# Sixteen first-table panels move into the stretch in which the gates are made

## The chip, the cores and the metric

The kernel runs on one core of one Trainium2 chip. The metric is the device time of one execution in microseconds (us). Engines by their names in the profile: PE is TensorE (PEld its weight loads), DVE VectorE, ACT ScalarE, POOL GpSimd, SP SyncE; SP and POOL also issue the DMA transfers.

## The reference

Two layers over 256 tokens of width 2048: a Conformer convolution with a SwiGLU block, then a block of forgetting attention and pooling, and last a product-key expert layer ("peer"). Only that last layer matters here:

```python
# per token and head: 16 experts out of 128*128, with gates
v1, i1 = lax.top_k(s1, 16); v2, i2 = lax.top_k(s2, 16)
cand = v1[..., :, None] + v2[..., None, :]
top_s, top_pos = lax.top_k(cand, 16)
gates = softmax(top_s)
# per token: 8 heads * 16 experts
u = take(expert_u, idx); a = einsum('thkd,td->thk', u, x)
hid = gelu(a) * g
out = einsum('thk,thkd->td', hid, take(expert_v, idx))
```

## The kernel before

The expert layer takes the last 1130 us or so of the run. The experts' first key splits the work in two.

**Sparse part, first keys 0 to 87.** For each of 16 (token half, head) routes and each of 16 slots, `gather_u` fetches one row of 8 KB per token for 128 tokens by an indirect DMA, `dot` (L1706, on DVE, two halves of 1024) multiplies it with the token, `gelu` and `hidden` (L1756) give the weight, `spreads` (L1050, on ACT) lays it out, `gather_v` fetches the second table's row and `adds` (L2292, on PE) accumulates it. Rows whose first key is 88 or more are not fetched. The slots go in 64 groups of four. The U rows have 5 buffers, the V rows 7. POOL issues both kinds from one program order: U of slot k, then V of slot k-4. The U gather waits until the dot of slot k-5 is done, the V gather until PE has used the buffer (`v_used`).

**Dense part, first keys 88 to 127.** These 40 blocks are computed for all tokens. `dense_u_panel(d)` (L2240, PE, 16 products of 128x128 by 128x256) makes the dots of one block from a 1 MB panel that SP loads into one of two buffers (`raw`), `dense_hidden(d)` (L1060, ACT) writes the gelu into a row of `ha`. The gates of these blocks are made from one-hot rows: ACT makes `one_keys`, DVE `one_keys_2` and `one_keys_late`, `token_four(f)` (L2280, PE) multiplies them four tokens at a time, and `gated(group)` (L1749, DVE) multiplies `ha` with the gates of eight tokens, over all 40 blocks at once. `dense_v_panel(d)` (L2250, PE) then multiplies by a 1 MB panel of the second table.

**Order.** It is written out by hand. PE runs an iteration i of 0 to 64, in which the `adds` are those of group i-1; DVE and ACT run the loop over g. The U panels pass in i = 0 to 16 (three in each of i = 0 and 1, then 34 over 15 iterations), the transposed slots at i = 17, the 64 fours of tokens at i = 18 to 31 (eight in each of 18 and 19, then four), the residual at 33, the V panels from i = 34 to 60, three in two iterations. DVE also has the routing (top-k, L1639 to L1686) of 13 routes in groups 0 to 15; the groups 4, 9 and 14 have none. In PE's iteration a first panel stands ahead of the `adds`, a second behind two of them. SP's queue after the last U panel holds `xn_late`, `xres_late` and the V panels in this order; the first waits until all 40 U panels were used (L470), since it overwrites their moving operand.

Of the kernel before, what the change touches and what calls it, by code (L numbers as in the profile page):

```python
# [35 lines left out]

DENSE = 40
GATE_TOKENS = 8
SPARSE = NKEYS - DENSE
RMS_EPS, LN_EPS = 1e-6, 1e-5  # L40
LOWEST = -3.0e38
# [86 lines left out]

def dense_block(d):

    return d + 16 if d < 24 else d - 16 if d < 32 else d - 32


def score_row(th):
# [21 lines left out]
def u_panels_in(i):  # L156

    if i < 2:
        return range(3 * i, 3 * i + 3)
    return range(6 + 34 * (i - 2) // 15, 6 + 34 * (i - 1) // 15) if i < 17 else range(0)  # L160


def token_fours_in(g):
# [51 lines left out]
def two_layers(nc, stream, dense_u, columns, x, meta, b_out, g_mix_post, g_ffn, g_ffn_post, g_norm1, g_norm2, w_forget,  # L215
# [144 lines left out]
    pick = place("s_pick", [128, 2 * TOPK * TOPK], pick_at)  # L360
    cand = place("s_cand", [128, TOPK * TOPK], pick_at)
    cand_rest = place("s_cand_rest", [128, TOPK * TOPK], pick_at + 4 * TOPK * TOPK)
    iota_i = small("s_iota_i", NKEYS, mybir.dt.int32)
    iota_f = small("s_iota_f", NKEYS)
    sc_rest = small("s_sc_rest", NKEYS)
# [17 lines left out]
    with ExitStack() as ctx:  # L383
# [56 lines left out]
        v_loaded = [sem(f"v_loaded{i}") for i in range(NV)]  # L440
        dot_ready, dots_added, gelu_ready, hid_ready = sem("dot_ready"), sem("dots_added"), sem("gelu_ready"), sem("hid_ready")
        spread_ready, v_used = sem("spread_ready"), sem("v_used")
        acc_done, out_ready, stored = sem("acc_done"), sem("out_ready"), sem("stored")

        def four_tiles(b):
# [171 lines left out]
        def _(act):  # L617
# [435 lines left out]

            def dense_hidden(d):

                b = 4 + d % 4
                act.wait_ge(panel_used, NPANELS + 1 + d + 1)
                if d == 32:
                    act.wait_ge(expert_ready, PH)
                act.activation(ha[:, dense_block(d), :], bank[b][:, 0:T], ACT.Gelu_apprx_tanh).then_inc(bank_empty[b], 1)  # L1060

            def slots_transposed(t):

# [17 lines left out]
                act.wait_ge(distance_ready, turn + 1)  # L1081
                act.activation(four, four, ACT.Relu, scale=-1.0, bias=1.0).then_inc(one_key_ready, 1)

            slots_stored = [n.after(f"empty{6 + t}", DENSE // 4 + 1) for t in range(TT)]
            for g in range(ROUTES * GROUPS):
                if g == 18:
                    for t in range(TT):
# [17 lines left out]
        def _(dve):  # L1105
# [614 lines left out]
            def one_keys_2(m):  # L1720

                if m == 0:
                    for t in range(TT):
                        dve.wait_ge(bank_empty[6 + t], n.after(f"empty{6 + t}", DENSE // 4 + 1))
                wait(dve, one_key_used, 2 * (m - 2))
                first = 8 * m % 128
                columns = [slots_t[m // 16][:, kind * SLOTS + first:kind * SLOTS + first + 8].unsqueeze(2).to_broadcast([128, 8, DENSE])
                           for kind in (0, 2)]
                eight = one_key_2[:, m % 3 * 8 * DENSE:(m % 3 + 1) * 8 * DENSE].rearrange("p (t g) -> p t g", t=8)
                link(dve.tensor_tensor(eight, iota_f[:, SPARSE:].unsqueeze(1).to_broadcast([128, 8, DENSE]), columns[0], ALU.is_equal))  # L1730
                dve.tensor_tensor(eight, eight, columns[1], ALU.mult).then_inc(one_key_2_ready, 1)
# [6 lines left out]
                dve.tensor_tensor(one_key_late[:, :].rearrange("p (t k) -> p t k", t=8),  # L1738
                                  iota_f[:, :].unsqueeze(1).to_broadcast([128, 8, NKEYS]), keys_2, ALU.is_equal).then_inc(one_key_late_ready, 1)

            def gated(group):

                b = 6 + group % 2
                if group == 0:
                    for a in range(2):
                        dve.wait_ge(bank_empty[4 + a], n.after(f"empty{4 + a}", DENSE // 4))
                dve.wait_ge(one_key_used, GATE_TOKENS // 4 * (group + 1))
                some = ha[:, :, GATE_TOKENS * group:GATE_TOKENS * (group + 1)]
                dve.tensor_tensor(some, some, bank[b][:, 0:GATE_TOKENS * DENSE].rearrange("p (t g) -> p g t", t=GATE_TOKENS), ALU.mult)\  # L1749
                    .then_inc(bank_empty[b], 1)  # L1750

            def hidden(g):

# [44 lines left out]
            for g in range(ROUTES * GROUPS):  # L1798
                for turn in range(BATCH):
                    dot(g * BATCH + turn)  # L1800
                    if turn == 0 and g:
                        hidden(g - 1)
                        if route_in(g - 1):
                            gates_softmax(route_in(g - 1))
                    if route_in(g):
                        route(route_in(g), turn)
                    fours = token_fours_in(g)
                    for f in fours[turn * len(fours) // 4:(turn + 1) * len(fours) // 4]:
                        if f >= 4 and f % 2 == 0:
                            gated(f // 2 - 2)  # L1810
                        if f % 2 == 0:
                            one_keys_2(f // 2)
                        if f % 4 == 1:
                            one_keys_late(f // 4)
                    if g == 32 and turn < 2:
                        gated(T // GATE_TOKENS - 2 + turn)
                dots_summed(g)
                if g == 61:
                    for q in range(4):
                        result(0, q)  # L1820
# [6 lines left out]
        def _(pe):  # L1827
# [399 lines left out]

            def dense_u_panel(d):

                b = 4 + d % 4  # L2230
                if d == 0:
                    pe.wait_ge(xnt_ready, 1)
                into(b, d // 4)
                if d < NE:
                    pe.wait_ge(early_loaded[d], 16)
                else:
                    pe.wait_ge(raw_loaded[(d - NE) % 2], (NPANELS // 4 + (d - NE) // 2 + 1) * 16)
                source = panel_early[d] if d < NE else raw[(d - NE) % 2]
                for k in range(KT):
                    ins = pe.matmul(bank[b][:, 0:T], source[:, k * 128:(k + 1) * 128], xnt[:, k, 0:T], start=k == 0, stop=k == KT - 1)  # L2240
                ins.then_inc(panel_used, 1)
# [14 lines left out]
            def slots_transposed(t):  # L2256

                pe.wait_ge(gates_ready, PH * (t + 1))
                into(6 + t, DENSE // 4)
                for kind in range(3):  # L2260
                    ins = pe.transpose(bank[6 + t][:, kind * SLOTS:(kind + 1) * SLOTS], picked[t][:, kind * SLOTS:(kind + 1) * SLOTS], ident[:, :])
                ins.then_inc(bank_full[6 + t], 1)

            def token_four(f):

                b = 6 + f // 2 % 2
                if f % 2 == 0:
                    into(b, DENSE // 4 + 1 + f // 4)
                turn = 2 * (f // 4) + f % 4
                if f % 4 < 2:  # L2270
                    pe.wait_ge(one_key_ready, turn + 1)
                else:
                    pe.wait_ge(one_key_late_ready, f // 4 + 1)
                pe.wait_ge(one_key_2_ready, f // 2 + 1)
                four = one_key[:, turn % 4 * 4 * NKEYS:(turn % 4 + 1) * 4 * NKEYS] if f % 4 < 2 else \
                    one_key_late[:, f % 2 * 4 * NKEYS:(f % 2 + 1) * 4 * NKEYS]
                for e in range(4):
                    token = 4 * f + e
                    own_2 = slice(token % 24 * DENSE, (token % 24 + 1) * DENSE)
                    ins = pe.matmul(bank[b][:, token % GATE_TOKENS * DENSE:(token % GATE_TOKENS + 1) * DENSE], four[:, e * NKEYS:(e + 1) * NKEYS],  # L2280
                                    one_key_2[:, own_2], start=True, stop=True)
                ins.then_inc(one_key_used, 1)
# [19 lines left out]
            for i in range(ROUTES * GROUPS + 1):  # L2302
                for d in u_panels_in(i)[:1]:
                    dense_u_panel(d)
                if i == 17:
                    for t in range(TT):
                        slots_transposed(t)
                if i == 33:
                    for b in (4, 5):
                        into(b, DENSE // 4)  # L2310
                    for b in (6, 7):
                        into(b, DENSE // 4 + 1 + T // GATE_TOKENS // 2)
                    pe.wait_ge(xres_back, 16)
                    residual(1)
                for d in v_panels_in(i)[:1]:
                    dense_v_panel(d)
                for f in token_fours_in(i)[:-4]:
                    token_four(f)
                for q in range(4):
                    if i >= 1:  # L2320
                        adds(4 * (i - 1) + q)
                    if q == 1:
                        for d in u_panels_in(i)[1:2]:
                            dense_u_panel(d)
                        for d in v_panels_in(i)[1:]:
                            dense_v_panel(d)
                for d in u_panels_in(i)[2:]:
                    dense_u_panel(d)
                for f in token_fours_in(i)[-4:]:
                    token_four(f)  # L2330
# [70 lines left out]
```

## Time and profile before

| | |
|---|---|
| median of 3 runs | 3005.09 us (3003.09 to 3007.17) |
| the profiled execution's own time | 3004.93 us |
| its span, first to last instruction | 3002.9 us |
| busy: PE, PEld | 2736.4, 2038.3 us |
| busy: DVE, ACT, POOL | 1923.8, 1178.5, 668.0 us |
| moved by DMA | 785.5 MB |

Each row of the profile's engine table is busy time of that engine in one execution. Busy PE is time with a matmul under way, whatever its clock; the granted clock is a row of its own, in tenths of full speed (2.4 GHz) in the slices and as a fraction in stretches. The DMA share is the mean busy share of the 16 DMA engines.

### The profile page before, as it was taken

The numbers are of one execution on the slowest core, as the hardware profiler recorded it, in microseconds if no ns is written. First come the engines' busy times: TensorE is split into PE (matmuls) and PEld (weight loads), VectorE is DVE, ScalarE is ACT, GpSimd is POOL, SyncE is SP. The second block draws the span as 40 slices with busy tenths as digits, with TensorE's granted clock in tenths as the row PEclk, the third lists the DMA queues.
The fourth block names the chain that finished last, engine by engine and source line by source line (L and its number), as shares of the span: only waits on it lengthen the run. The fifth ranks groups of instructions, "written<-read, shape, count | busy, mean of one in ns | idle before, by whom it ended". The sixth has DMA issues, their size and how long they took to land.

```text
span 3002.9 us, 45413 instructions
## 1 busy us (share of the span) xinstructions
PE 2736.4 (91%) x17100; PEld 2038.3 (68%) x17100; DVE 1923.8 (64%) x3184; ACT 1178.5 (39%) x2298; POOL 668.0 (22%) x568
## 2 busy tenths in 40 slices
PE   8999999999999998999999999999976678888884
PEld 7886788888888887989999889777753322222220
DVE  6888566555656565455445558987769875555555
ACT  1003443334333344425334444645456642222232
POOL 0000000000000000040000002544448765454453
PEclk9999999999999998999999999999977779999886
DMA  6333545555555553443555657999999999999997
GB/s 244 140 141 111 206 157 185 187 191 183 194 182 193 184 192 122 155 152 141 182 182 182 248 199 250 372 418 408 415 375 408 397 409 417 409 420 391 411 409 300
DMA packets 131297, 785.51 MB, mean 262 GB/s; under 512 B 34630, under 2 KB 34630, under 8 KB 35846
## 3 DMA queue, kind: packets, MB, share of 16 engines
q1 hardware_dynamic: 55424, 393.68, 35.5%
q0 software_dynamic: 75712, 389.74, 32.3%
q8 instruction: 93, 1.52, 0.2%
q14 instruction: 68, 0.56, 0.1%
HBM read 940.23 MB, written 4.19 MB: 315 GB/s over the span
## 4 chain that ended last, share of the span: by engine, by line
PE 57%; DMA 20%; DVE 12%; issue 6%; ACT 3%; POOL 1%; DVEq 1%; POOLq 0%; SPq 0%; ACTq 0%
DMA s_u<-in_expert_u,s_u_index 17%; PE bank L1847 10%; PE bank L1841 10%; PE bank L1843 10%; PE bank L1842 10%; PE bank L1848 5%; PE bank L1937 4%; DVE s_u L1706 4%; PE bank L2240 4%; PE bank L2292 2%; DMA s_v<-in_expert_v,s_v_index 2%; DVE s_cacc L1217 2%; ACT s_spread L1050 2%; DVE s_w_lo L1128 1%; DVE s_yrow L1390 1%
## 5 line engine op out<-in xcount | busy, mean ns | idle before, releaser
L1128 DVE TENSOR_TENSOR s_w_lo<-s_raw,s_w_hi 128x2048 fp32r<-128x2048 f32 x258 | 592.6, 2297 | 577.8 <-ACT s_w_hi L628 577.4
L628 ACT ACTIVATE s_w_hi<-s_raw 128x2048 fp32r<-128x2048 f32 x256 | 490.5, 1916 | 750.9 <-PE bank L1843 475.4
L1847 PE MATMUL bank<-s_a,s_w_hi 128*128 128x512 f32 x1408 | 494.7, 394 | 3.2 <-DVE s_w_lo L1128 3.2
L2292 PE MATMUL bank<-s_v,s_spread 128*32 128x512 f32 x2048 | 302.8, 721 | 183.1 <-ACT s_spread L1050 115.9
L1706 DVE CUSTOM_DVE_ANT_0 s_u<-s_u,s_xn_late 128x1024 f32<-128x1024 f32 x256 | 303.8, 1224 | 246.8 <-DMA s_u<-in_expert_u,s_u_index 246.5
L1050 ACT ACTIVATE s_spread<-s_ident,s_hid 32x32 f32<-32x32 f32 x1024 | 325.6, 318 | 205.5 <-DVE s_hid L1756 188.0
L1848 PE MATMUL bank<-s_a,s_w_lo 128*128 128x256 f32 x1408 | 395.1, 281 | 0.0
L585 POOL DMA_INDIRECT s_u<-in_expert_u,s_u_index x256 | 300.0, 1172 | 416.4 <-DVE s_halfdot L1706 240.4
L601 POOL DMA_INDIRECT s_v<-in_expert_v,s_v_index x256 | 317.9, 1242 | 196.8 <-PE bank L2292 115.5
L1706 DVE CUSTOM_DVE_ANT_0 s_u<-s_u,s_xn 128x1024 f32<-128x1024 f32 x256 | 303.8, 1224 | 60.3 <-DMA s_u<-in_expert_u,s_u_index 59.3
L1841 PE MATMUL bank<-s_a,s_w_hi 128*128 128x256 f32 x1152 | 325.1, 282 | 3.4 <-DVE s_a L1152 1.8
L1842 PE MATMUL bank<-s_a,s_w_hi 128*128 128x256 f32 x1152 | 324.4, 282 | 0.0
L1843 PE MATMUL bank<-s_a,s_w_lo 128*128 128x256 f32 x1152 | 324.0, 281 | 0.0
L2292 PEld LDWEIGHTS bank<-s_v,s_spread 128*32 128x32 f32 x2048 | 62.9, 125 | 375.5 <-ACT s_spread L1050 135.4
L1847 PEld LDWEIGHTS bank<-s_a,s_w_hi 128*128 128x128 f32 x1408 | 264.7, 188 | 66.5 <-DVE s_w_lo L1128 6.4
L2250 PE MATMUL bank<-s_raw,s_ha 128*32 128x512 f32 x2560 | 295.5, 615 | 0.0
L2240 PE MATMUL bank<-s_xnt,s_raw 128*128 128x256 f32 x1184 | 264.7, 382 | 2.1 <-DMA s_raw<-in_dense_u 2.1
L1848 PEld LDWEIGHTS bank<-s_a,s_w_lo 128*128 128x128 f32 x1408 | 265.0, 188 | 0.4
L2240 PEld LDWEIGHTS bank<-s_xnt,s_raw 128*128 128x128 f32 x1184 | 222.1, 190 | 58.7 <-issue 29.1
L1937 PE MATMUL bank<-s_a_f,s_raw 128*128 128x272 f32 x1024 | 235.2, 393 | 2.9 <-DVE s_a_f L1185 2.1
L2250 PEld LDWEIGHTS bank<-s_raw,s_ha 128*32 128x32 f32 x2560 | 83.3, 115 | 215.1 <-issue 215.1
L1937 PEld LDWEIGHTS bank<-s_a_f,s_raw 128*128 128x128 f32 x1024 | 194.4, 190 | 43.4 <-issue 3.5
(321 smaller groups left out, 3809.8 us busy)
## 6 DMA issues: line engine op xcount, KB each, us to landing
s_raw<-in_stream SPq DMA_DIRECT2D x292, 1024.0 KB, 4.7
s_raw<-in_expert_v SPq DMA_DIRECT2D x40, 1024.0 KB, 8.9
s_raw<-in_dense_u SPq DMA_DIRECT2D x37, 1024.0 KB, 8.7
s_u<-in_expert_u,s_u_index POOLq DMA_INDIRECT x256, 17.4
s_v<-in_expert_v,s_v_index POOLq DMA_INDIRECT x256, 17.6
s_panel_early<-in_dense_u POOLq DMA_DIRECT2D x3, 1024.0 KB, 11.5
s_xres<-in_x SPq DMA_DIRECT2D x2, 1024.0 KB, 6.0
out<-s_out_row SPq DMA_DIRECT2D x32, 64.0 KB, 3.3
```

Source lines behind the costliest of these rows:

```text
L628: act.activation(w_hi[s % 2][:, :], raw[s][:, :], ACT.Copy).then_inc(hi_ready, 1)
L1050: ins = act.activation(spread[g % NW][s * Q:(s + 1) * Q, q, :], ident[own, own], ACT.Copy, scale=hid[g % NH][own, s:s + 1])
L1128: dve.tensor_tensor(w_lo[s % 2][:, :], raw[s][:, :], w_hi[s % 2][:, :].bitcast(f32), ALU.subtract)\
L1706: ins = dve.tensor_tensor_reduce(out=u_slot[k % NU][:, half], in0=u_slot[k % NU][:, half], in1=xn_late[:, half] if t else xn[:, 0, half], ...
L1841: pe.matmul(dst, left[0], right[0], start=start, stop=False)
L1842: pe.matmul(dst, left[0], right[1], start=False, stop=False)
L1843: return pe.matmul(dst, left[1], right[0], start=False, stop=stop)
L1847: pe.matmul(dst, left[0], both, start=start, stop=False)
L1848: return pe.matmul(dst[:, 0:T], left[1], both[:, 0], start=False, stop=stop)
L1937: ins = pe.matmul(bank[c][:, 0:L], raw[c % 4][:, k * 128:(k + 1) * 128], a_f[:, k, :], start=k == 0, stop=k == KT - 1)
L2240: ins = pe.matmul(bank[b][:, 0:T], source[:, k * 128:(k + 1) * 128], xnt[:, k, 0:T], start=k == 0, stop=k == KT - 1)
L2292: ins = pe.matmul(bank[4 * t + q][c * Q:(c + 1) * Q, :], spread[g % NW][:, q, :], v_slot[k % NV][:, c * 512:(c + 1) * 512], start=False, s ...
```

## The change

The first 24 panels pass in i = 0 to 16, the other 16 in i = 17 to 29, at 16 over 13 iterations. They use banks 4 and 5 alone, since banks 6 and 7 hold the gates by then. The gates of a group of tokens may now come before the gelu of some panels: `gated(group, missing)` copies the gates into those rows of `ha` (the late panels are rows 0 to 15, the last panel row 0) and multiplies the rest. When a late panel's gelu comes, ACT writes the tokens whose gates are already in place into one of two buffers `late_act`, the other tokens straight into `ha`, and DVE's `landed(d)` multiplies the two, at the first turn of group i+2.

```diff
+FIRST_U, LATE_U = 24, 16
...
     if i < 2:
         return range(3 * i, 3 * i + 3)
-    return range(6 + 34 * (i - 2) // 15, 6 + 34 * (i - 1) // 15) if i < 17 else range(0)
+    if i < 17:
+        return range(6 + (FIRST_U - 6) * (i - 2) // 15, 6 + (FIRST_U - 6) * (i - 1) // 15)
+    return range(FIRST_U + LATE_U * (i - 17) // 13, FIRST_U + LATE_U * (i - 16) // 13) if i < 30 else range(0)
...
+def u_bank(d):
+
+    if d < FIRST_U:
+        return 4 + d % 4, d // 4
+    return 4 + (d - FIRST_U) % 2, FIRST_U // 4 + (d - FIRST_U) // 2
+
+
+def gated_before(g):
+
+    fours = 8 * (g - 18) if g < 20 else 4 * (g - 16)
+    return max(0, min(fours, T // 4) // 2 - 2)
+
+
+LANDS_IN = {d: i + 2 for i in range(30) for d in u_panels_in(i) if d >= FIRST_U}
...
-                b = 4 + d % 4
+                b, late = u_bank(d)[0], d - FIRST_U
                 act.wait_ge(panel_used, NPANELS + 1 + d + 1)
-                if d == 32:
-                    act.wait_ge(expert_ready, PH)
-                act.activation(ha[:, dense_block(d), :], bank[b][:, 0:T], ACT.Gelu_apprx_tanh).then_inc(bank_empty[b], 1)
+                done = 0
+                if late >= 0:
+                    done = GATE_TOKENS * gated_before(LANDS_IN[d])
+                    if late == 0:
+                        act.wait_ge(expert_ready, TT * PH)
+                    wait(act, late_landed, late - 1)
+                    act.activation(late_act[:, late % 2, 0:done], bank[b][:, 0:done], ACT.Gelu_apprx_tanh)
+                act.activation(ha[:, dense_block(d), done:], bank[b][:, done:T], ACT.Gelu_apprx_tanh).then_inc(bank_empty[b], 1)
...
-                dve.tensor_tensor(some, some, bank[b][:, 0:GATE_TOKENS * DENSE].rearrange("p (t g) -> p g t", t=GATE_TOKENS), ALU.mult)\
-                    .then_inc(bank_empty[b], 1)
+                gates = bank[b][:, 0:GATE_TOKENS * DENSE].rearrange("p (t g) -> p g t", t=GATE_TOKENS)
+                if missing:
+                    dve.tensor_copy(some[:, 0:missing, :], gates[:, 0:missing, :])
+                dve.tensor_tensor(some[:, missing:, :], some[:, missing:, :], gates[:, missing:, :], ALU.mult).then_inc(bank_empty[b], 1)
+
+            def landed(d):
+
+                late, (b, k) = d - FIRST_U, u_bank(d)
+                groups = gated_before(LANDS_IN[d])
+                for group in (groups - 2, groups - 1):
+                    gates_taken = n.after(f"empty{6 + group % 2}", FIRST_U // 4 + 2 + group // 2)
+                    dve.wait_ge(bank_empty[6 + group % 2], gates_taken)
+                dve.wait_ge(bank_empty[b], n.after(f"empty{b}", k + 1))
+                some = ha[:, dense_block(d), 0:GATE_TOKENS * groups]
+                dve.tensor_tensor(some, some, late_act[:, late % 2, 0:GATE_TOKENS * groups], ALU.mult).then_inc(late_landed, 1)
...
-                    fours = token_fours_in(g)
+                    for d in range(FIRST_U, DENSE):
+                        if turn == 0 and LANDS_IN[d] == g:
+                            landed(d)
+                    fours, missing = token_fours_in(g), sum(LANDS_IN[d] > g for d in range(FIRST_U, DENSE))
                     for f in fours[turn * len(fours) // 4:(turn + 1) * len(fours) // 4]:
                         if f >= 4 and f % 2 == 0:
-                            gated(f // 2 - 2)
+                            gated(f // 2 - 2, missing)
```

The other edits set the banks' counts to the new number of panels. The two table layouts follow `dense_block`, so each panel is still 1 MB, and as many are loaded.

## Rows read from the trace of the kernel before

**Rows 1.** The page's 40 slices: PE, its granted clock, the DMA engines.
```profile
PE   8999999999999998999999999999976678888884
PEclk9999999999999998999999999999977779999886
DMA  6333545555555553443555657999999999999997
```
**Rows 2.** Windows over groups 2-15, 16-33 and 34-60: length, busy, clock, DMA.
```profile
core 0: us, PE busy (x) PEld busy (x) DVE busy (x) ACT busy (x) POOL busy (x), PEclk, DMA share, GB/s
1891.72:2169.78 278.06, 275.93 (x1460) 201.30 (x1453) 230.26 (x649) 152.53 (x490) 134.40 (x113) 1.00 1.00 411
2169.78:2450.03 280.25, 197.35 (x1248) 111.70 (x1250) 233.31 (x441) 162.99 (x493) 184.48 (x143) 0.74 0.98 396
2450.03:2932.43 482.40, 402.30 (x3416) 107.86 (x3412) 263.43 (x486) 142.94 (x459) 249.24 (x216) 0.91 1.00 410
```
**Rows 3.** Timeline of DVE: last instruction of groups 1 to 4, 20, 21 (start, us).
```profile
1891.72 0.16 DVE L1718 TENSOR_TENSOR s_adot<-s_halfdot 128x4 f32<-128x4 f32 x1
1911.78 0.15 DVE L1718 TENSOR_TENSOR s_adot<-s_halfdot 128x4 f32<-128x4 f32 x1
...
1931.85 0.15 DVE L1718 TENSOR_TENSOR s_adot<-s_halfdot 128x4 f32<-128x4 f32 x1
...
1941.83 0.17 DVE L1718 TENSOR_TENSOR s_adot<-s_halfdot 128x4 f32<-128x4 f32 x1
...
2263.94 0.16 DVE L1718 TENSOR_TENSOR s_adot<-s_halfdot 128x4 f32<-128x4 f32 x1
...
2277.20 0.17 DVE L1718 TENSOR_TENSOR s_adot<-s_halfdot 128x4 f32<-128x4 f32 x1
```
**Rows 4.** The chain that ended last, 1928 to 1937 us (start, us, what).
```profile
1928.00 7.10 PE bank L2240 x32
1935.11 1.85 PE bank L2292 x16
```
**Rows 5.** DMA by queue and issue: first 1850 to 1890 us, then 1890 to 2200.
```profile
s_u<-in_expert_u,s_u_index POOLq DMA_INDIRECT x8, 8.6
s_v<-in_expert_v,s_v_index POOLq DMA_INDIRECT x6, 6.4
...
q0 software_dynamic: 17815, 90.80, 71.7%
q1 hardware_dynamic: 4896, 35.65, 27.9%
...
s_u<-in_expert_u,s_u_index POOLq DMA_INDIRECT x64, 19.2
```
**Rows 6.** Timeline of PE, 2200 to 2254 us: the same work at both clocks.
```profile
2200.58 3.64 PE L2292 MATMUL bank<-s_v,s_spread 128*32 128x512 f32 x32
...
2223.90 5.50 PE L2292 MATMUL bank<-s_v,s_spread 128*32 128x512 f32 x32
...
2242.25 3.61 PE L2280 MATMUL bank<-s_one_key,s_one_key_late 128*128 128x40 f32 x16
...
2252.33 1.96 PE L2280 MATMUL bank<-s_one_key,s_one_key_late 128*128 128x40 f32 x16
```
**Rows 7.** Windows of 5 us (columns as in Rows 2), and a line of POOL's timeline.
```profile
2245.00:2250.00 5.00, 5.00 (x36) 1.79 (x36) 4.10 (x7) 0.00 (x0) 1.39 (x1) 0.68 0.48 195
2250.00:2255.00 5.00, 4.29 (x40) 3.65 (x32) 4.93 (x12) 1.86 (x7) 3.27 (x4) 1.00 0.74 241
...
2248.61 1.66 POOL L601 DMA_INDIRECT s_v<-in_expert_v,s_v_index  x1 [6.45 <-PE bank L2292]
```
**Rows 8.** Groups by line, 1850 to 3003 us (busy us, mean ns | idle before).
```profile
L1738 DVE TENSOR_TENSOR s_one_key_late<-s_iota_f,s_slots_t 128x1024 f32<-128x1024 f32 x16 | 19.5, 1219 | 2.6 <-PE bank L2280 2.6
L1749 DVE TENSOR_TENSOR s_ha<-s_ha,bank 128x320 f32<-128x320 f32 x32 | 15.4, 481 | 3.2 <-PE bank L2280 3.2
L1060 ACT ACTIVATE s_ha<-bank 128x256 f32<-128x256 f32 x40 | 13.4, 382 | 9.6 <-PE bank L2240 9.3
```

More of the change, by code:

```diff
@@ L129, in dense_block @@
 def dense_block(d):
-    return d + 16 if d < 24 else d - 16 if d < 32 else d - 32
+    return d + LATE_U if d < FIRST_U else DENSE - 1 - d
 def score_row(th):
@@ L362, in two_layers @@
     cand_rest = place("s_cand_rest", [128, TOPK * TOPK], pick_at + 4 * TOPK * TOPK)
+    late_act = place("s_late_act", [128, 2, T], pick_at)
     iota_i = small("s_iota_i", NKEYS, mybir.dt.int32)
@@ L442, in two_layers @@
         spread_ready, v_used = sem("spread_ready"), sem("v_used")
+        late_landed = sem("late_landed")
         acc_done, out_ready, stored = sem("acc_done"), sem("out_ready"), sem("stored")
@@ L1082, in one_keys @@
                 act.activation(four, four, ACT.Relu, scale=-1.0, bias=1.0).then_inc(one_key_ready, 1)
-            slots_stored = [n.after(f"empty{6 + t}", DENSE // 4 + 1) for t in range(TT)]
+            slots_stored = [n.after(f"empty{6 + t}", FIRST_U // 4 + 1) for t in range(TT)]
             for g in range(ROUTES * GROUPS):
@@ L1723, in one_keys_2 @@
                     for t in range(TT):
-                        dve.wait_ge(bank_empty[6 + t], n.after(f"empty{6 + t}", DENSE // 4 + 1))
+                        dve.wait_ge(bank_empty[6 + t], n.after(f"empty{6 + t}", FIRST_U // 4 + 1))
                 wait(dve, one_key_used, 2 * (m - 2))
@@ L1739, in one_keys_late, with gated @@
                                   iota_f[:, :].unsqueeze(1).to_broadcast([128, 8, NKEYS]), keys_2, ALU.is_equal).then_inc(one_key_late_ready, 1)
-            def gated(group):
+            def gated(group, missing):
                 b = 6 + group % 2
@@ L1745, in gated @@
                     for a in range(2):
-                        dve.wait_ge(bank_empty[4 + a], n.after(f"empty{4 + a}", DENSE // 4))
+                        dve.wait_ge(bank_empty[4 + a], n.after(f"empty{4 + a}", FIRST_U // 4))
                 dve.wait_ge(one_key_used, GATE_TOKENS // 4 * (group + 1))
                 some = ha[:, :, GATE_TOKENS * group:GATE_TOKENS * (group + 1)]
-                dve.tensor_tensor(some, some, bank[b][:, 0:GATE_TOKENS * DENSE].rearrange("p (t g) -> p g t", t=GATE_TOKENS), ALU.mult)\
-                    .then_inc(bank_empty[b], 1)
+                gates = bank[b][:, 0:GATE_TOKENS * DENSE].rearrange("p (t g) -> p g t", t=GATE_TOKENS)
[11 more added lines that the diff above has]
+                dve.tensor_tensor(some, some, late_act[:, late % 2, 0:GATE_TOKENS * groups], ALU.mult).then_inc(late_landed, 1)
             def hidden(g):
@@ L1815, in _ @@
                     if g == 32 and turn < 2:
-                        gated(T // GATE_TOKENS - 2 + turn)
+                        gated(T // GATE_TOKENS - 2 + turn, 0)
                 dots_summed(g)
@@ L2228, in dense_u_panel @@
             def dense_u_panel(d):
-                b = 4 + d % 4
+                b, k = u_bank(d)
                 if d == 0:
                     pe.wait_ge(xnt_ready, 1)
-                into(b, d // 4)
+                into(b, k)
                 if d < NE:
@@ L2258, in slots_transposed @@
                 pe.wait_ge(gates_ready, PH * (t + 1))
-                into(6 + t, DENSE // 4)
+                into(6 + t, FIRST_U // 4)
                 for kind in range(3):
@@ L2267, in token_four @@
                 if f % 2 == 0:
-                    into(b, DENSE // 4 + 1 + f // 4)
+                    into(b, FIRST_U // 4 + 1 + f // 4)
                 turn = 2 * (f // 4) + f % 4
@@ L2309, in _ @@
                     for b in (4, 5):
-                        into(b, DENSE // 4)
+                        into(b, FIRST_U // 4 + LATE_U // 2)
                     for b in (6, 7):
-                        into(b, DENSE // 4 + 1 + T // GATE_TOKENS // 2)
+                        into(b, FIRST_U // 4 + 1 + T // GATE_TOKENS // 2)
                     pe.wait_ge(xres_back, 16)
```

## The prediction

> **What bounds the kernel now.** I read the slices first, then the windows, then the timelines inside them. The slices show the expert layer (the last 15) with the DMA row at 9 and PE's clock down after 2200 us [rows 1]. The change touches two stretches of it. *Front*, groups 2 to 15, 278.06 us; *middle*, groups 16 to 33, 280.25 us. The third, groups 34 to 60, it leaves alone. The windows show a DMA share of 1.00, 0.98 and 1.00 in the three [rows 2]. PE is busy for 275.93 of 278.06 us in the front, and for 197.35 of 280.25 at a granted clock of 0.74 in the middle. DVE stands at 230 and 233 us.
>
> So three resources are close in the front. Each alone would take:
> - PE: back to back, a panel 7.10 us and the 16 products behind it 1.85 [rows 4]. Per group 31/14 panels and 32 `adds` products: 2.21 x 7.10 + 3.7 = 19.4 us. It is nearly the 19.9 us that a group lasts (278.06 / 14).
> - DVE: groups 1 to 3, all with routing, last 20.06 us each; group 4, without, 9.98 [rows 3]. Groups 2 to 15 have 11 with routing and 3 without (4, 9, 14): 220.7 + 29.9 = 250.6 us.
> - DMA: queue q1 moved 35.65 MB, 34 panels of 1.05 MB, in 4896 packets, 144 each, for 27.9% of 310 us: 2.54 us of all 16 engines per panel. Queue q0 had 17815 packets, at 144 each 123.7 gathers, for 71.7%: 1.80 us per gather, 14.4 us per group of eight [rows 5]. Front: 14 x 14.4 + 31 x 2.54 = 280.3 us against 278.06 measured. Middle: 18 x 14.4 + 7 x 2.54 (three U panels, xn_late, xres_late, two V panels) = 277.0 against 0.98 x 280.25 = 274.6. The working closes to 1%.
>
> DMA thus explains the length of both stretches; PE explains the front as well, but not the middle.
>
> **The change, part by part.**
> *Transfers.* Nothing is removed: as many gathers and as many 1 MB panels. Of 31 U panels in the iterations of the front 16 stay; 15 x 2.54 = 38.1 us of transfer go to the middle (there 3 become 18). If DMA never idled before or after, the end would not move at all. What counts is idle DMA.
>
> *Front.* DMA's work falls to 278 - 38 = 240 us, PE's to 14 x 3.7 + 16 x 7.10 = 165 us. DVE's stays at 250.6 and is now the largest: the front can't be shorter than that, and it gets DVE for its bound. I take 253, since groups differ. While DVE is the bound, DMA gets ahead, but only as far as the buffers go. How far, I read from issue to landing: 19.2 us under a full queue, 8.6 us just before, at 1850 to 1890, where DVE paced the groups [rows 5]. The queue holds 19.2 - 8.6 = 10.6 us less at the front's end: that much of the transfers is done earlier. 240 + 10.6 = 250.6, as much as DVE needs; so DMA idles for some 2 us only.
>
> *Middle.* 274.6 + 38.1 - 10.6 = 302.1 us of transfer, plus idle. Before, idle was 2% of 280, 5.6 us, most of it in one place: the V gather at 2248.61 was held 6.45 us by PE, and the share was 0.48 and 0.74 in the two 5 us windows there [rows 7]. PE was late because it had waited for the first one-hot rows and then worked at half clock. With a panel in each of those iterations PE fills that wait and its clock may hold: 16 L2280 products take 1.96 us at full and 3.61 at half clock, 32 L2292 3.64 and 5.50 [rows 6]. That would give 2 to 3 us back. Against it, the four 1 MB transfers that followed the last U panel are no longer there to fill the gap, and PE is tighter. I take 6 us of idle: 308 us.
>
> *PE in the middle.* Per group of 18 to 29: 32 L2280 products 3.9, `adds` 3.7, 16/13 panels 8.7, together 16.3 us, against DMA's 14.4 + 1.23 x 2.54 = 17.5. It fits at full clock, with 1.2 us to spare.
>
> *DVE in the middle.* At its own pace a group there takes it 13.26 us (group 21) [rows 3]. From the two widths 1024 in 1219 ns and 320 in 481 ns [rows 8], an operation costs about 0.15 us fixed and 1.05 ns per element. `landed` runs 16 times over 16 to 224 tokens, 2128 elements in all: 16 x 0.15 + 2.2 = 4.6 us, with its waits some 6. Splitting `gated` adds the fixed part 28 times: 4.2 us. The sum is 10 us over 13 groups, 0.8 each: 14.1, under 17.5; free while DMA paces. `landed` stands at the first turn of group i+2 and waits for ACT's gelu of a panel that PE passed in iteration i. Behind it stand the next dot, the gates and, through `dot_ready`, POOL's gathers. PE runs panel i before the `adds` of i-1, which themselves wait for group i on DVE, so it has about a group (17 us) in hand: nothing, unless PE falls behind. The overwritten buffer (`late_landed`) is freed in the same turn in which ACT needs it; under 1 us of ACT.
>
> *ACT.* 16 more gelus, at most 0.38 each [rows 8], 6 us over 13 groups; ACT is busy 163 of 280 us [rows 2]. Free.
>
> *Queues.* SP: sixteen loads come later, and behind them xn_late, xres_late and the first two V panels. The last U panel passes in iteration 29, xn_late is needed in group 32; two groups (35 us) against 19.2 us of landing at worst [rows 5]. Free. POOL's order is untouched.
>
> *Sum.* 253 + 308 = 561 against 558.3 now: +2.7 us. On the profiled execution (span 3002.9, its time 3004.93) that is 3007.6; the median of the runs is 0.16 above it, so **3007.8**. Bounds: with no lead over from the front, the middle has 312.7 + 6 and the sum is +13.4. With a larger lead (17 us) the front itself becomes DMA's, 257, and the sum +0.4; with no idle left, -5.6.
>
> **The rivals.**
> *A, PE is what bounds the front, and the middle has room.* For it: PE's 99% of the front at full clock, 70% of the middle. The front falls by 27.4 us to DVE's 250.6; the middle takes the panels in at less than their 2.54 us, because its clock and its order leave DMA 396 GB/s where the front had 411 [rows 2]. At 411 the middle's transfers need 3.6% less, 10 us; then the sum is +2.7 - 10, minus some idle: 2994. Against it: 0.98 share already. The Trainium skill's "Perfetto Trace Analysis" (Optimization Strategy) says that a kernel whose most-contended engine changes over time may gain by interleaving the regimes; by that rule this case comes out. The rows of the share say that the most-contended one is DMA on both sides.
> *B, PE becomes the bound of the middle (slower).* Half clock costs it 14.3 us per group (30.6 against 16.3, with a panel at twice 7.10), so it passes DMA's 17.5 once over 8% of its work runs at half clock. It then holds V gathers, and POOL with them U gathers, as at 2248.61. For it: the clock was 0.74 in the middle and 0.91 in the last stretch, where PE was busy 402 of 482 us [rows 2]. Against it: there DMA kept its share of 1.00, and a PE that is behind has no wait in which its clock falls. At 15% of its work: 18.4 us per group, 13 x 0.9 = 12 us more: 3020. The skill's "TensorE: Matmul & The Clock Gate" (HAM oscillation) says that waits between bursts of products throw the array back to the low clock again and again; by it the front, where PE would now wait as well, could fall to half clock too, and the granted clock of after will show whether it does.
> *C, DVE bounds the front and the lead is lost.* 253 us with DMA idle in them, the middle 318.7: 3018.
>
> **How the numbers follow.** Forecast 0.50, at 3007.8 (2999 to 3012 by itself); A 0.17 at 2994; B 0.20 at 3020; C 0.13 at 3018. A measurement of this kernel can tell about 0.2%, 6 us, from no change: 2999 to 3011. Faster is A, 0.17. Same is most of the forecast and a little of C, 0.48. Slower is B, the rest of C and of the forecast, 0.35. The range runs from A's time to B's: 2994 to 3020.
>
> **What the profile of after would show.** Right: groups with routing in the front at 20.1 us, the others at 10 to 12, group 15 ending near 2145 us; DMA share a little under 1.00 there and landings of gathers well under 19 us; PE at two thirds; in the middle groups of 17 to 18 us at a share of 0.98; group 33 ending within 6 us of 2450; the last stretch as it was. Wrong: a share under 0.95 in the front (C); waits of V gathers for PE and a share under 0.96 in the middle (B); over 411 GB/s in the middle (A). What would overturn all of it is a gather's cost that itself depends on what runs beside it.

## The result and the profile after

The changed kernel takes 3014.27 us in the median (3010.58 to 3017.27) against 3005.23 (3003.09 to 3007.17) for the kernel before beside it: a ratio of 1.0031, 95% interval 1.0020 to 1.0042. It is 9 us slower. That is inside the range of the prediction (2994 to 3020), but not its forecast of +2.7, and above the 3011 from which on the prediction itself spoke of slower, at a chance of 0.35.

The same three stretches as in [rows 2], cut at the ends of the same groups (1, 15, 33, 60), in windows of the changed kernel (columns as in [rows 2]):

```profile
1891.14:2142.17 251.03, 192.13 (x1023) 121.01 (x1016) 230.09 (x649) 148.21 (x476) 132.90 (x113) 0.89 0.99 394
2142.17:2459.54 317.37, 278.38 (x1688) 194.99 (x1691) 238.15 (x484) 169.28 (x523) 178.82 (x143) 0.89 0.98 396
2459.54:2943.91 484.37, 406.15 (x3408) 107.72 (x3404) 263.49 (x487) 142.98 (x459) 246.60 (x216) 0.89 1.00 410
```

The front is 27.0 us shorter (251.03 for 278.06), the middle 37.1 longer (317.37 for 280.25), the last stretch 2.0 longer. The front's length is DVE's: of its last two groups the one without routing takes 10.00 us and the one with it 19.97, both as in [rows 3]. In the timeline of DVE the ends of groups 13, 14 and 15 (start, us):

```profile
2112.20 0.16 DVE L1744 TENSOR_TENSOR s_adot<-s_halfdot 128x4 f32<-128x4 f32 x1
2122.20 0.17 DVE L1744 TENSOR_TENSOR s_adot<-s_halfdot 128x4 f32<-128x4 f32 x1
2142.17 0.16 DVE L1744 TENSOR_TENSOR s_adot<-s_halfdot 128x4 f32<-128x4 f32 x1
```

What DMA brought in during the front, in the changed kernel and then, for comparison, in the kernel before (queue: packets, MB, share of the 16 engines; issues: count, us to landing):

```profile
q0 software_dynamic: 15680, 79.95, 80.1%
q1 hardware_dynamic: 2554, 18.69, 18.5%
s_v<-in_expert_v,s_v_index POOLq DMA_INDIRECT x57, 11.9
s_u<-in_expert_u,s_u_index POOLq DMA_INDIRECT x56, 11.1
```
```profile
q0 software_dynamic: 15796, 80.59, 70.9%
q1 hardware_dynamic: 4558, 33.27, 29.0%
s_v<-in_expert_v,s_v_index POOLq DMA_INDIRECT x57, 17.6
s_u<-in_expert_u,s_u_index POOLq DMA_INDIRECT x56, 19.2
```

At 144 packets each these are 108.9 gathers after and 109.7 before: no lead at the front's end, though a gather now lands in 11 us, not in 19. Panels: 17.7 for 31.7, 13.9 fewer (2004 packets). At the 2.54 us of [rows 5] they are worth 35.3 us; the front gained 27.0 of them. The middle has 13.9 panels more, 35.3 us, and grew by 37.1. By this account 8.3 of the 10.1 us by which front and middle together grew are lost in the front, 1.8 in the middle.

The middle shows a new wait, in the changed kernel's waits from 2150 to 2460 us (us in total, times, longest):

```profile
POOL s_u L606 <- DVE s_halfdot L1732: 49.2, 24, 5.6
POOL s_v L622 <- PE bank L2334: 47.4, 16, 8.0
DVE s_ha L1777 <- PE bank L2322: 36.7, 9, 11.5
```

In the last line DVE, at the start of `gated`, waits for PE's fours; in the kernel before that was 3.2 us in all [rows 8]. The wait falls on the groups behind the three iterations with two panels. Group 22, from the timelines of PE, DVE and POOL:

```profile
2249.36 7.17 PE L2282 MATMUL bank<-s_xnt,s_raw 128*128 128x256 f32 x32
2256.46 1.92 PE L2334 MATMUL bank<-s_v,s_spread 128*32 128x512 f32 x16
2258.32 1.98 PE L2322 MATMUL bank<-s_one_key,s_one_key 128*128 128x40 f32 x16
...
2260.33 0.26 DVE L1777 COPY s_ha<-bank 128x96 f32<-128x96 f32 x1 [9.28 <-PE bank L2322]
...
2264.95 1.15 POOL L606 DMA_INDIRECT s_u<-in_expert_u,s_u_index  x1 [5.55 <-DVE s_halfdot L1732]
```

PE passes the second panel (2249.36) ahead of the fours of tokens (L2322); `gated` on DVE waits 9.28 us for them, and the dots and with them the U gathers wait behind it. The group takes 23.0 us, where its neighbours take 13.6 and 14.7. So there were two suspects: the floor that DVE sets in the front, and this wait.

### The profile page after: what moved, and what is told of

The parts are those of the page before. It is cut to its first block, busy times and chain, and to the rows that moved or that the text cites. A ratio compares the mean times of both kernels' runs of the same rounds, so it can differ in the third digit from the quotient of the medians.

```text
span 3013.1 us, 45503 instructions
## 1 busy us (share of the span) xinstructions
PE 2736.4 (91%) x17100; PEld 2040.5 (68%) x17100; DVE 1928.6 (64%) x3228; ACT 1180.4 (39%) x2314; POOL 659.5 (22%) x568
## 4 chain that ended last, share of the span: by engine, by line
PE 58%; DVE 16%; DMA 15%; issue 6%; ACT 4%; DVEq 1%; POOL 1%; POOLq 0%; SPq 0%; ACTq 0%
DMA s_u<-in_expert_u,s_u_index 13%; PE bank L1889 10%; PE bank L1883 10%; PE bank L1885 10%; PE bank L1884 10%; DVE s_u L1732 5%; PE bank L1890 5%; PE bank L1979 4%; PE bank L2282 4%; PE bank L2334 2%; DVE s_cacc L1243 2%; PE bank L2322 2%; DMA s_v<-in_expert_v,s_v_index 2%; ACT s_spread L1071 1%; DVE s_w_lo L1154 1%
## 5 line engine op out<-in xcount | busy, mean ns | idle before, releaser
L2334 PE MATMUL bank<-s_v,s_spread 128*32 128x512 f32 x2048 | 291.5, 699 | 208.0 <-ACT s_spread L1071 125.6
L606 POOL DMA_INDIRECT s_u<-in_expert_u,s_u_index x256 | 293.6, 1147 | 474.7 <-DVE s_halfdot L1732 310.5
L1732 DVE CUSTOM_DVE_ANT_0 s_u<-s_u,s_xn 128x1024 f32<-128x1024 f32 x256 | 303.1, 1223 | 31.8 <-DMA s_u<-in_expert_u,s_u_index 30.6
L1889 PEld LDWEIGHTS bank<-s_a,s_w_hi 128*128 128x128 f32 x1408 | 264.3, 188 | 66.6 <-DVE s_w_lo L1154 6.4
L2292 PE MATMUL bank<-s_raw,s_ha 128*32 128x512 f32 x2560 | 301.0, 625 | 0.0
L2282 PE MATMUL bank<-s_xnt,s_raw 128*128 128x256 f32 x1184 | 273.6, 390 | 0.6 <-DMA s_raw<-in_dense_u 0.6
L2282 PEld LDWEIGHTS bank<-s_xnt,s_raw 128*128 128x128 f32 x1184 | 228.3, 195 | 54.7 <-issue 22.8
L2292 PEld LDWEIGHTS bank<-s_raw,s_ha 128*32 128x32 f32 x2560 | 83.9, 116 | 219.2 <-issue 218.6
L1883 PEld LDWEIGHTS bank<-s_a,s_w_hi 128*128 128x128 f32 x1152 | 218.1, 189 | 8.5 <-issue 4.4
```

Of the source, the lines that this page charges most:

```text
L1732: ins = dve.tensor_tensor_reduce(out=u_slot[k % NU][:, half], in0=u_slot[k % NU][:, half], in1=xn_late[:, half] if t else xn[:, 0, half], ...
L1883: pe.matmul(dst, left[0], right[0], start=start, stop=False)
L1889: pe.matmul(dst, left[0], both, start=start, stop=False)
L2292: ins = pe.matmul(bank[4 * t + q][c * Q:(c + 1) * Q, :], ha[:, d, t * 128 + q * Q:t * 128 + (q + 1) * Q], raw[r][:, c * 512:(c + 1) * 512] ...
L2334: ins = pe.matmul(bank[4 * t + q][c * Q:(c + 1) * Q, :], spread[g % NW][:, q, :], v_slot[k % NV][:, c * 512:(c + 1) * 512], start=False, s ...
```

## Experiments

All times are medians; the ratio is to the kernel before, run beside it on the same chip.

**1. The second panel behind the fours.**

```diff
-                    if q == 1:
-                        for d in u_panels_in(i)[1:2]:
+                    if q == 1:
+                        for d in u_panels_in(i)[1:2] if i < 17 else ():
                             dense_u_panel(d)
...
                 for f in token_fours_in(i)[-4:]:
                     token_four(f)
+                for d in u_panels_in(i)[1:2] if i >= 17 else ():
+                    dense_u_panel(d)
```

> The changed kernel with one move: in iterations 21, 25 and 29, the three with two late panels, PE passes the second panel behind the fours of tokens, not ahead of them. Order theory (in these iterations the fours come about 7 us late, DVE's gated waits 9.3, 5.8 and 11.5 us for them, and the dots, the U gathers and DMA wait behind it): those waits go, groups 22, 26 and 30 fall from 23.0, 19.5 and 25.2 us to about 17, and the time falls from 3014 to 3004 to 3009 (part comes back as later adds, since two panels now stand in a row ahead of them). Work theory (PE simply has too much to do in the middle, whatever the order): the same work, so 3012 to 3016, with the waits at another instruction.

3011.16 us, 1.0020 (1.0010 to 1.0029). Groups 22, 26 and 30 fell to 16.7, 15.5 and 17.9 us, but the groups behind them rose (23 to 20.0, 27 to 21.5, 31 to 21.2), and the middle ends up at 316.39 us, 1 less. The time lies between the two expectations. By the medians order is worth some 3 us of the 9, but the interval overlaps that of the changed kernel (1.0020 to 1.0042), so it may be nothing.

**2 to 4. Fewer late panels, and twelve in pairs.** The number is the constant; so that no gelu overwrites an early panel's buffer, the rows of `ha` are dealt out anew.

```diff
-FIRST_U, LATE_U = 24, 16
+FIRST_U, LATE_U = 28, 12        # 32, 8 in the third
...
-    return d + LATE_U if d < FIRST_U else DENSE - 1 - d
+    return d + 16 if d < 24 else d - 24 + LATE_U if d < FIRST_U else DENSE - 1 - d
...
# pairs only
-    return range(FIRST_U + LATE_U * (i - 17) // 13, FIRST_U + LATE_U * (i - 16) // 13) if i < 30 else range(0)
+    return range(FIRST_U + 2 * ((i - 17) // 2), FIRST_U + 2 * ((i - 16) // 2)) if i < 30 else range(0)
```

> 12 late panels, one in each of iterations 18 to 29, and 28 early ones; so no iteration of the middle has two. Order theory: no long wait of gated, 3000 to 3005. Work theory: 4 of 16 panels less, so about three quarters of the 9 us stay, 3009 to 3013. Idle theory (DMA starves in the DVE-bound front): DMA needs 250 us there, as much as DVE, so hardly any idle is left and the time is that of before, 3003 to 3006.

> The same 12 late panels, but two in each of iterations 18, 20, 22, 24, 26 and 28 and none between. Same work, same transfers, same front as with one in each. Order theory: gated waits some 6 to 11 us in the six groups behind those iterations, half of it comes back in the iterations without a panel: slower than one in each by 8 to 25 us, 3012 to 3028. Work theory and idle theory: as with one in each, within 3 us.

> 8 late panels (iterations 18 to 29, never two in one) and 32 early. Order theory: no long wait of gated; the front is bound by DMA again, so 3001 to 3006, about the time of before. Work theory: half of the 9 us, 3008 to 3011. Idle theory: 3003 to 3006.

Twelve singly: 3009.05 us, 1.0014 (1.0005 to 1.0023). Twelve in pairs: 3017.47, 1.0039 (1.0026 to 1.0053). Eight: 3012.43, 1.0022 (1.0013 to 1.0031). Front and middle of each, in this order (windows):

```profile
1890.76:2145.08 254.32, 209.53 (x1099) 139.89 (x1092) 230.01 (x650) 149.53 (x480) 128.83 (x110) 0.91 0.99 399
2145.08:2453.40 308.32, 265.22 (x1613) 177.16 (x1615) 238.10 (x480) 167.70 (x515) 178.89 (x145) 0.86 0.99 400
```
```profile
1892.79:2146.15 253.36, 210.41 (x1103) 140.73 (x1096) 229.99 (x649) 149.54 (x480) 127.11 (x110) 0.92 0.99 402
2146.15:2461.76 315.61, 271.82 (x1601) 181.15 (x1603) 236.38 (x478) 167.15 (x515) 182.01 (x145) 0.84 0.98 390
```
```profile
1890.49:2151.34 260.85, 228.74 (x1208) 158.08 (x1204) 229.93 (x649) 150.31 (x483) 127.31 (x110) 0.95 1.00 404
2151.34:2459.56 308.22, 251.73 (x1502) 161.08 (x1498) 237.50 (x476) 166.20 (x508) 181.32 (x145) 0.80 0.97 388
```

Pairs cost 8.4 us over singles with the same work (the middle 7.3), and the wait of `gated` is 43.3 us in all there, 6.6 with singles. So the grouping can cost what the order theory said, at the lower end of its range. Twelve singly lose 3.4 us: more than the order theory had (3005 at most), and just at the lower edge of the work theory (3009 to 3013), which the pairs then refute. Eight fit no theory (3011 at most). Counted in packets the front has 7.7 panels fewer (3456 for 4558), 19.4 us, and is 17.2 us shorter; the middle has as many more and is 28.0 us longer, at 388 GB/s where it had 396. Some 4 us of this lie in groups 18 and 19, where the gates begin: they last 45.1 us at a DMA share of 0.82, which leaves 8.1 us idle, where the kernel before and the changed one leave 4.3 and 4.1 (share 0.91).

**5 to 8. Transfers or products taken out.** In the changed kernel on the 16 late panels, in the kernel before on every other panel of iterations 2 to 16:

```diff
# not loaded: one row in place of 128
-                sp.dma_start(raw[r][:, :], src).then_inc(raw_loaded[r], 16)
+                rows = slice(0, 1) if FIRST_U <= d < DENSE else slice(0, 128)
+                sp.dma_start(raw[r][rows, :], src[rows, :]).then_inc(raw_loaded[r], 16)
...
# one product: the first of 16
-                for k in range(KT):
+                kept = 1 if d >= FIRST_U else KT
+                for k in range(kept):
...
# in the kernel before the condition is 7 <= d < 38 and d % 2 == 1
```

> The changed kernel, but of the 16 late panels only one row of 128 is loaded (8 KB in place of 1 MB), so their dots are of old data; PE, ACT and DVE do all they did. The middle then has 16 x 2.54 = 41 us less of transfer. If DMA alone sets the middle's length: 2975 to 2980. If PE's order and amount of work hold it (16.3 us a group at full clock, gated's waits in groups 22, 26 and 30 unchanged): a good part of the 41 us isn't had, 2985 to 2998, and those three groups stay above 20 us.

> The changed kernel, but of each late panel's 16 products PE does only the first; all is loaded, and ACT and DVE work as before on the partial dots. PE has 107 us less in the middle, so no wait of gated or of a V gather for PE is left there. Order theory: 4 to 6 us of the 9 go, 3007 to 3010. If the rest is what the front lost (DVE-bound, with no lead in gathers at its end), it is still slower than before by 2 to 6 us. Were PE all of the cause, it would be at 3005 or under.

> The kernel before, but of every other U panel from the 7th to the 37th (16, all of iterations 2 to 16) only one row is loaded; all else is done. DMA in the front falls by 38 to 240 us. If PE's 19.4 us a group bound it as well: the front falls by only 6 to 9 us, 2995 to 3000. If DMA alone was the bound: down to DVE's 250.6, so 2976 to 2980.

> The kernel before, but of the same 16 U panels PE does only the first of 16 products; all is loaded. PE in the front falls by 100 us. If DMA bound it as well (280 us of transfer in 278): no change beyond 3 us, 3001 to 3006. If PE alone was the bound: down to DVE's, 2976 to 2982.

First the kernel before. Half the products gone: 3005.82, 1.0005 (0.9996 to 1.0015), no change. Half the loads gone: 2994.69, 0.9967 (0.9956 to 0.9979), 10 of 41 us. Their fronts, products first:

```profile
1893.20:2170.01 276.81, 202.60 (x990) 131.63 (x982) 230.47 (x650) 152.49 (x490) 132.47 (x110) 0.87 0.99 405
```
```profile
1893.01:2156.93 263.92, 262.64 (x1393) 191.22 (x1385) 230.62 (x650) 153.05 (x490) 127.22 (x106) 1.00 0.93 356
```

With PE busy for 73 us less the front stays at 277 us: DMA alone is enough to hold it there. Without the loads DVE ends its groups after 264 us, but that is not a floor of PE that lies 14 us lower. PE's own panel products in the two fronts, before and with half the loads gone (columns: length, busy, clock, DMA share, GB/s), and its last early panel in both:

```profile
1891.72:2169.78 278.06, 226.03 (x1012) 1.00 1.00 411
1893.01:2156.93 263.92, 214.62 (x961) 1.00 0.93 356
```
```profile
2192.39 7.17 PE L2240 MATMUL bank<-s_xnt,s_raw 128*128 128x256 f32 x32
2192.74 7.17 PE L2241 MATMUL bank<-s_xnt,s_raw 128*128 128x256 f32 x32
```

PE did 51 records less there, 1.6 panels (a panel has 32), and came to its last early panel 300.7 us after the front's start in the first and 299.7 in the second. So PE needs the same time for its part whether DMA is relieved or not; only DVE ran ahead of it, and it kept some of that through the opening of the gates: group 18 ends 337.1 us after the front's start in the kernel before and 327.7 without the loads, 9.4 us sooner. DMA and PE thus both bound the front at about the length it has, each alone being enough; DVE's 250.6 us come next, some 27 us below. The change relieves both of the first two.

Then the changed kernel. Late panels not loaded: 2995.07, 0.9972 (0.9961 to 0.9983), 19 us under the changed kernel for 41 us of transfer. Late panels with one product: 3016.92, 1.0045 (1.0028 to 1.0061), nothing gained, which no expectation had. Their middles:

```profile
2143.46:2437.33 293.87, 269.46 (x1681) 187.99 (x1684) 237.64 (x484) 169.25 (x523) 182.24 (x143) 0.91 0.95 369
```
```profile
2141.28:2458.96 317.68, 221.40 (x1209) 122.73 (x1211) 239.37 (x485) 169.11 (x523) 176.37 (x143) 0.68 0.98 397
```

Without the loads the second case of its expectation came: the middle falls by 23.5 us and not by 41, PE is busy for 269.5 of its 293.9 us, and groups 22, 26 and 30 stay at 21.5 us each. Its last fours of tokens come 22.3 us sooner too, counted from the middle's start. So PE's work and its order hold the middle next, some 23 us under the length that it has.

With the products gone, `gated` waits 10.1 us in all instead of 36.7, and the middle is as long as it was (317.68 for 317.37), 397 GB/s for 396. That speaks against the wait as the cause, with one reservation: PE's clock fell to 0.68, the opening of the gates (groups 18 and 19) grew from 45.9 to 50.5 us, and what came behind (groups 20 to 33) shrank from 238.4 to 236.5. The waits of the changed kernel are thus worth some 2 us by these groups. That they mostly stand where the gathers would have been late anyway is my reading of it, not measured.

**9, 10 and 12. DVE lighter in the front**, in the changed kernel and in the one before, beside the changed kernel unedited. It leaves out most of every other dot's second half in groups 2 to 15:

```diff
-                    half = slice(h * D // 2, (h + 1) * D // 2)
+                    width = 64 if 2 <= g < 16 and s % 2 and h else D // 2
+                    half = slice(h * D // 2, h * D // 2 + width)
```

> The changed kernel with DVE made lighter in the front: in groups 2 to 15 the second half of every other dot covers 64 of its 1024 columns (about 1.0 us less each, 28 of them, 28 us; the dots are then incomplete). The front's floor on DVE falls from 250.6 to about 223 us, under DMA's 240. Floor theory (what the change loses is the 10 us by which DVE's floor in the front stands above what the transfers left there need): the front ends 8 to 11 us earlier than in the changed kernel and the time is that of the kernel before, 3002 to 3007. If the loss is made in the middle (gated's waits, PE's order or clock): at most 3 us better than the changed kernel, 3010 to 3015.

> The kernel before with the same lighter DVE in groups 2 to 15. There the transfers need 280 us, DVE 250.6: nothing is to be had. Floor theory: within 3 us of the kernel before, 3002 to 3008. If lighter dots were worth something by themselves (and the run above so no test of the floor): 2995 or less.

> The changed kernel itself, unedited, beside the three others on the same chip: 3012 to 3016, for a paired comparison with the lighter DVE.

Changed, unedited: 3014.34, 1.0033 (1.0020 to 1.0045). Changed, DVE lighter: 3008.58, 1.0010 (1.0001 to 1.0019). Before, DVE lighter: 3005.03, 1.0003 (0.9994 to 1.0012). The front of the first two, unedited and lighter, and what q0 did in it:

```profile
1892.08:2142.91 250.83, 190.98 (x1017) 119.64 (x1010) 229.91 (x649) 148.20 (x476) 133.99 (x112) 0.88 0.99 392
q0 software_dynamic: 15658, 79.83, 80.2%
```
```profile
1891.65:2136.67 245.02, 195.94 (x1017) 121.99 (x1010) 202.29 (x650) 148.21 (x476) 126.60 (x113) 0.90 1.00 406
q0 software_dynamic: 15741, 80.31, 80.7%
```

5.8 us come back in the front with DVE's work alone (250.8 to 245.0). The middle is 317.3 us there; it was 317.4 in the changed kernel's first profile and 319.4 in the unedited one beside it, whose profiled execution took 3019.11 us, 5 above its median. The same edit is worth nothing in the kernel before. The time is just above what the floor theory gave (3002 to 3007), so the floor carries about 6 of the 9.5 us, not all.

**11. Four late panels, where the gates begin.** `FIRST_U, LATE_U = 36, 4`, rows dealt out as above, with a wait for the first eight routes ahead of the gelu of panel 24, and

```diff
-    return range(FIRST_U + LATE_U * (i - 17) // 13, FIRST_U + LATE_U * (i - 16) // 13) if i < 30 else range(0)
+    return range(FIRST_U + i - 17, FIRST_U + i - 16) if i < 21 else range(0)
```

> Only four late panels, one in each of iterations 17 to 20, where the gates begin and DMA idles for 5 us in the kernel before; 36 early ones. The front then keeps more transfer than DVE's floor (4 x 2.54 = 10 us less of 278), so nothing is lost there by the floor theory; in the gap PE has a panel in each iteration and DMA its load. If the gap closes by half: 3001 to 3004. If it doesn't, and the front's three bounds just trade places: 3004 to 3008.

3007.84 us, 1.0011 (1.0002 to 1.0020): the second case. The front (3.0 panels fewer by packets, 7.7 us) is 8.8 us shorter, the middle 11.9 longer. The gap that it was to close is wider, in windows of 5 us:

```profile
2220.00:2225.00 5.00, 5.00 (x44) 2.72 (x37) 4.96 (x12) 0.21 (x1) 3.56 (x3) 0.95 0.54 192
2240.00:2245.00 5.00, 5.00 (x45) 2.56 (x37) 4.96 (x12) 0.20 (x1) 3.26 (x3) 0.91 0.42 116
```

PE is busy and at a high clock there, and DMA still has little to do: two windows under 0.6 where the kernel before has one [rows 7]. The four 1 MB transfers that follow the last U panel, and that fill this place before, come only after it. No version with late panels beat the kernel before.

## Why the prediction was right or wrong

**The bounds of the kernel before: right.** DMA explains the length of the front and PE explains it as well: the two runs with work taken out show that each is enough (277 us without half the products; PE's panels done at the same time without half the loads). Rival A (PE bounds the front, the middle has room) is refuted in both halves: the front doesn't move without PE's products, and the middle ran at 396 GB/s after as before.

**The front: right.** DVE became its bound. 253 us forecast, 251.0 measured, with groups of 20.1 and 10.0 us and group 15 ending at 2142.

**The lead: wrong, and this is the step that failed.** The prediction took 10.6 us of transfer as done early, from landings of 19.2 against 8.6 us. The landings did fall, to 11.1, but 108.9 gathers had landed at the front's end against 109.7 before. In both kernels 113 were issued in the front, since a U gather waits for a dot and a V gather stands behind it in POOL's order. A landing time says how long one transfer is under way, not how far the queue has run ahead. The 10.6 us also came from medians over long stretches, while near the front's end stands group 14, without routing: DVE passes it in 10.0 us, and DMA needs 14.4 for its eight gathers. In the 20 us behind that group the changed kernel's landings (U, then V) are up again:

```profile
s_u<-in_expert_u,s_u_index POOLq DMA_INDIRECT x6, 13.5
s_v<-in_expert_v,s_v_index POOLq DMA_INDIRECT x7, 12.9
```

The sum of the prediction with no lead was +13.4; rival C had this mechanism, at 0.13. Measured between the profiles is +10.1, since the front came out 2.0 us under the 253 and the middle 1.3 under the 318.7. The range held this because it reached up to rival B's time, and B did not happen: that the result lies inside it is in part luck.

**Idle of the middle: about right.** 6 us taken; a share of 0.98 over 317.37 us leaves 6.3. Transfers for 35.3 us more (the prediction had 38.1, whole panels by iteration), length 37.1 more. The gap at the start of the gates stayed; the gain and the loss that I had set against each other there both appear (PE's clock over groups 18 and 19 is 0.85 where it was 0.64, and they take 45.9 us for 47.7; four transfers are gone from the gap), and the run with four late panels, whose middle grew by 4.2 us more than its panels are worth, shows the loss.

**DVE's new work: right.** In the changed kernel's middle `landed` is busy for 4.7 us (4.6 worked out), and `gated` for 13.1 and 6.5 us in its two parts, 4.2 more than the 15.4 of before (4.2 worked out). Groups 20 and 21, whose `landed` is among the shortest, take 13.49 and 13.58 us for 13.28 and 13.26, and no run shows a cost of it.

**The wait of `landed`: right, but the wrong wait was looked at.** DVE has no idle time ahead of it (16 times, 0.0 us). What the prediction left out is that `gated` waits for the fours, and that in the iterations with two panels these stand behind both. The profile makes much of it (36.7 us), the runs little: some 2 to 3 us, not clear of noise. With twelve panels in pairs it is worth 8.

**Rival B (PE bounds the middle): no.** V gathers do wait more for PE (47.4 us for 20.0), but with the late panels' products gone (PE busy for 57 us less, at a lower clock) the middle is as long. The price of half clock in this rival was also read too low: the 5.50 us of 32 L2292 products in [rows 6] began at a granted clock of 0.50 and ended at 0.92, so they are not the price at half clock, and the sum of the figures used is 30.2 us, not 30.6. Neither changes the forecast. The clock in the front fell from 1.00 to 0.89 once PE had waits there. That is what the Trainium skill's "TensorE: Matmul & The Clock Gate" (HAM oscillation) says of waits between bursts, and the trace agrees; no cost of it shows there: the groups kept DVE's 20.1 and 10.0 us, with PE idle for 59 us.

**What stays open.** Some 2 us of the front's loss with DVE lighter too (245.0 against 278.1 - 35.3 = 242.8), and the 3.8 us by which that run is still slower than the kernel before. Why eight late panels lengthen the middle by 28.0 us for 19.4 us of panels, beyond the 4 us in groups 18 and 19. Why the wait of `gated` costs 8 us in pairs of twelve and hardly any in the changed kernel.

## What to carry to other kernels

Where one resource is busy throughout, moving work in time gains only what that resource idled, and can lose more: count first how far the place that is relieved can shrink before the next engine stops it, and compare that with what the other place grows by. Here the front could give up 27 us and the middle had to take on 35. A run with one resource relieved is read by where the other's own work ends, not only by the stretch: a neighbour may have run ahead. A look-ahead that hangs on buffers is the same at both ends of a stretch; count what landed, not how fast.

## What the runs showed that was not expected

**DMA's share doesn't show that it has time.** In the changed kernel's front the share is 0.99, yet taking work from DVE let the same transfers through in 6 us less. The engines' time per gather moves instead: 80.1% of 251.03 us over 108.9 gathers is 1.85 us, with DVE lighter 80.7% of 245.02 over 109.3 is 1.81, in the kernel before 70.9% of 278.06 over 109.7 is 1.80. At 1850 to 1890 us, at 275 GB/s and landings of 8.6 us, it is 2.25 us (72.5% of 40 us, 1855 packets) in the kernel before. In these rows a gather costs the engines the more time the emptier the queue is, and the share counts that as busy. GB/s (394, 406, 411) showed what the share hid; that is why rival C's mark, a share under 0.95, never appeared though its mechanism did.

**A low clock of PE shows in the time in one place only.** With the late panels' products gone, the middle's granted clock was 0.68 for 0.89, and groups 18 and 19, where DVE and DMA both hang on PE's first fours, took 4.6 us longer (clock 0.60 there, for 0.85); the groups behind them were no slower.
